# Another order on the way to the first expert, the gates spread by GpSimd, and the next tokens' low parts between two weight low parts

## The chip, the cores and the metric

The kernel runs on one core of a Trainium2 chip. The metric is the device time of one execution in microseconds (us); lower is better. The engines are TensorE (PE, with PEld for its weight loads), VectorE (DVE), ScalarE (ACT), GpSimd (POOL) and SyncE (SP), which here only issues transfers.

## The reference

One layer of a decoder over 1024 tokens of 1024 channels, in float32. Two mixers (an RG-LRU and an S5 scan), a cross-attention into 256 memory tokens, then a mixture of experts: each token goes to its top 4 of 32 experts, each a clamped SwiGLU with weights of 1024x2048 and 1024x1024.

```
logits = xt @ router_w + router_b
top_val, top_idx = lax.top_k(logits, TOP_K)
gates = jax.nn.softmax(top_val, axis=-1)
...
def clamped_swiglu_expert(xb, w_gu, b_gu, w_down, b_down):
    gu = xb @ w_gu + b_gu
    g, u = gu[:, :D_FF], gu[:, D_FF:]
    ...
    h = (u + 1.0) * (g * jax.nn.sigmoid(SWIGLU_ALPHA * g))
    return h @ w_down + b_down
...
y = jnp.zeros((n, d), xt.dtype).at[slot_tok].add(yb.reshape(n_slots, d) * slot_w[:, None])
```

## The kernel before

Every engine has its own program, written out by hand in the order in which it runs; semaphores alone join them. A matrix product of the experts is done in three passes over float32r parts: ACT casts a weight tile of 1 MB to its high part (WH), DVE subtracts to get the low part (WL, `low_weights`), and TensorE multiplies high by high, low by high and high by low. Tokens are treated alike: TensorE transposes them into PSUM, ACT keeps the high part (XEH, `keep_tokens`), DVE the low part (XEL, `low_tokens`); the hidden rows give HTH and HTL (`low_hidden`).

**The loop** runs over items, of which 36 have work. An item is one expert's gate/up product for up to 128 tokens (one tile), or 192 (two tiles, a wide expert), together with the down product of the item before. TensorE's order in one turn is: four pairs of gate/up passes (the bias matmul L976 opens each pair, then L984, L988), the first half of the next tokens' transposes (L942), two down parts (L1005, L1012), the second half of the next tokens' transposes, the hidden transposes of half 0 (L1037), two down parts, the hidden transposes of half 1. The latter write the PSUM banks in which the second half of the next tokens stood, so they wait for `xel_done`, DVE's low part of that half. The next turn's first matmul is L976, which waits for `htl_done`, the hidden rows' low part of half 0. The loop is two loops, one of four turns inside another (`items`).

At the turn's end DVE does, in this order: low weight 8, low weight 9 (the next expert's first two gate/up tiles), the next tokens' second half, the hidden rows' low part of half 0, low weights 10 and 11. SP loads a weight tile into a slot when `gu_low` says that the low part of the tile in it is done.

**The way to the first expert.** After the last router product DVE works out the slots: the item list (ITM, which every engine waits for as `itm_done`), the positions, a one-hot of their rows (OHR, 128x3072; ACT scales it in eight parts into IDR), a one-hot of their columns (OHC, `slot_columns`), which TensorE multiplies with IDR into the list of tokens by slot (`list_done`), and the gates (GF: softmax weights spread over the experts, 128x256). GF goes to DRAM by SP (`gf_done`), ahead of SP's loop; GF3 is three copies of it, for the very end. The low weights 1 to 3 stand in the place of OHC and IDR, so they wait for the list. TensorE's program starts its loop behind the evacuation of the last bank (EBS), the first tokens' transposes and the list.

Of the kernel before, what the change touches and what calls it, by code (L numbers as in the profile page):

```python
# [13 lines left out]
F32 = mybir.dt.float32  # L14
# [7 lines left out]
P = 128  # L22
# [7 lines left out]
def build(nc, A, out):  # L30
    D = A["w_in"].shape[0]
    T = A["x"].shape[1]
    L = T // P
# [11 lines left out]
    TOPK = 4  # L45
# [14 lines left out]
    with ctx:  # L60
# [3 lines left out]
        def sem(name):  # L64
            return ctx.enter_context(nc.semaphore(name))
# [192 lines left out]
        def raw_gu(j):  # L258
            return raw((j + 2) % 6)
# [105 lines left out]
        def units_read(eng, kind):  # L365
# [30 lines left out]
        gexp_in, gexp_done, gf_done, gf_out = sem("gexp_in"), sem("gexp_done"), sem("gf_done"), sem("gf_out")  # L396
        hot0_done, idx0_done, idr_done, list_done, tab_done = (
            sem("hot0_done"), sem("idx0_done"), sem("idr_done"), sem("list_done"), sem("tab_done"))
        ohr_done, rw_done = sem("ohr_done"), sem("rw_done")
        acc_out, ids_done, gs_in = sem("acc_out"), sem("ids_done"), sem("gs_in")  # L400
        ms_done, itm_done, ite_done = sem("ms_done"), sem("itm_done"), sem("ite_done")
        hot_done, idx_done = sem("hot_done"), sem("idx_done")
# [668 lines left out]
        def _(act):  # L1071
# [244 lines left out]
            def keep_tokens(half, tiles):  # L1316
                for t in range(tiles):
                    n = HP if t else P
                    ins = nc.scalar.copy(XEH[:, 4 * half:4 * half + 4, t * P:t * P + n],
                                         PS[:, 2 * half + t, :].rearrange("p (k s) -> p k s", k=4)[:, :, 0:n])  # L1320
                ins.then_inc(xeh_done, 1)

            act.sem_inc(dn_high, 4)
            act.wait_ge(ohr_done, 1)
            for l in range(L):
                hot = OHR.rearrange("p (j l) r -> p j l r", l=L)[:, :, l, :]
                nc.scalar.activation(IDR[l // 4][:, :, l % 4, :], hot, ACT.Copy, scale=TOKF[:, l:l + 1]).then_inc(idr_done, 1)
            for half in range(2):
                act.wait_ge(xt_filled, half + 1)
                keep_tokens(half, 2)  # L1330
            act.wait_ge(gf_done, 1)
            nc.scalar.copy(GF3.rearrange("p l (r e) -> p l r e", r=3), GF.unsqueeze(2).to_broadcast([P, L, 3, E])) \
                .then_inc(gf3_done, 1)
            act.wait_ge(itm_done, 1)
            counts = Counts(act, "act")
            with items(act, counts, each=True) as i:
# [131 lines left out]
        def _(dve):  # L1468
# [392 lines left out]
            for t in range(2):  # L1861
                if t:
# [35 lines left out]
            d(v.tensor_reduce(K0[:, 3:4], IT2, AX.X, add))  # L1898
            ts(K0[:, 3:4], K0[:, 3:4], float(E - 1), None, ALU.min)
            ts(DIAG, ident[:], K0[:, 3:4], None, mul, s=ite_done)  # L1900
            tt(OHS, OH, SL.unsqueeze(1).to_broadcast([P, TOPK, L * E]), mul)
            d(v.tensor_reduce(POSf, OHS.rearrange("p j (l e) -> p (j l) e", l=L), AX.X, add))
            ts(PRW, POSf, 1.0 / P, 0.5 / P - 0.5, mul, add)
            ts(PRW, PRW, 1.5 * 2 ** 23, None, add)
            ts(PRW, PRW, 1.5 * 2 ** 23, None, sub)
            stt(PCL, PRW, -float(P), POSf, mul, add)
            dve.wait_ge(acc_out, 16 * (L + 1))
            v.tensor_tensor(OHR, PRW.unsqueeze(2).to_broadcast([P, TOPK * L, NROW]),
                            IOF[:, 0:NROW].unsqueeze(1).to_broadcast([P, TOPK * L, NROW]), ALU.is_equal).then_inc(ohr_done, 1)
            wait_filled(dve, ("itm",))  # L1910
            evac(dve, v.tensor_copy(ITM3[:, 0:2, 1:P + 1],
                                    bank(("itm",))[0:1, 0:2 * P].rearrange("o (r c) -> o r c", r=2)), ("itm",), own=True)
            dve.sem_inc(itm_done, 1)
            wait_filled(dve, ("eb",))
            evac(dve, v.tensor_copy(EBS, bank(("eb",))[:, 0:NROW]), ("eb",), own=True)
            def slot_columns(h):
                ns = slice(2 * L * h, 2 * L * (h + 1))
                v.tensor_tensor(OHC[:, ns, :], PCL[:, ns].unsqueeze(2).to_broadcast([P, 2 * L, P]),
                                IOF[:, :].unsqueeze(1).to_broadcast([P, 2 * L, P]), ALU.is_equal).then_inc(hot_done, 1)

            def gates():
                dve.wait_ge(gexp_done, 1)
                d(v.tensor_reduce(MXT[:, 0:L], GW, AX.X, add))
                d(v.reciprocal(MXT[:, 0:L], MXT[:, 0:L]))
                tt(GW, GW, MXT[:, 0:L].unsqueeze(2).to_broadcast([P, L, TOPK]), mul)
                for j in range(TOPK):
                    tt(GT1 if j else GF, OH4[:, j], GW[:, :, j:j + 1].to_broadcast([P, L, E]), mul)
                    if j:
                        tt(GF, GF, GT1, add, s=gf_done if j == TOPK - 1 else dve_step)

            def low_tokens(half, tiles):
                for t in range(tiles):
                    n = HP if t else P
                    o = XEH[:, 4 * half:4 * half + 4, P + HP:W] if t else XEL[:, 4 * half:4 * half + 4, 0:P]
                    hi = XEH[:, 4 * half:4 * half + 4, t * P:t * P + n].bitcast(F32)
                    ins = v.tensor_tensor(o, PS[:, 2 * half + t, :].rearrange("p (k s) -> p k s", k=4)[:, :, 0:n], hi, sub)
                ins.then_inc(xel_done, 1)

            def low_weights(s, src, done):
                v.tensor_tensor(WL[:, s, :], src, WH[:, s, :].bitcast(F32), sub).then_inc(done, 1)  # L1940

            dve.sem_inc(dn_low, 8)
            dve.sem_inc(htl_done, 2)
            for j in range(4):
                dve.wait_ge(gu_high, j + 1)
                low_weights(j, raw_gu(j), gu_low)
                if j == 0:
                    slot_columns(0)
                    slot_columns(1)
                    for half in range(2):  # L1950
                        dve.wait_ge(xeh_done, half + 1)
                        low_tokens(half, 2)
                    gates()
                    dve.wait_ge(list_done, 1)
                    ts(IDXF, PS[:, 7, 0:NROW], 1.0, 0.0, sub, ALU.max)
                    d(v.tensor_copy(IDX[:, 0:NROW], IDXF), idx_done)
            ts(SCF, PS[:, 7, 0:NROW], 0.5, DUM, ALU.is_lt, mul)
# [5 lines left out]
            with items(dve, counts) as i:  # L1963
# [87 lines left out]

                def weights_and_tokens(tiles):
                    gate_up_low(8)
                    gate_up_low(9)
                    next_tokens(1)(tiles)

                def no_tokens():
                    last_low(0)
# [40 lines left out]
        def _(pool):  # L2099
# [112 lines left out]
            pool.sem_inc(ys_free, 1)  # L2212
            pool.sem_inc(y_done, 1)
            g.tensor_copy(SELR[:, 0:P], SELT[:, 0:1].to_broadcast([P, P])).then_inc(sel_done, 1)
            pool.wait_ge(itm_done, 1)
            n_1 = entry(pool, 1, 2, W)
            pool.wait_ge(xt_filled, 2)
# [73 lines left out]
```

## Time and profile before

| | us |
|---|---|
| median of 3 runs | 2253.53 (2251.64 to 2256.22) |
| the profiled execution: its span, from first to last instruction | 2253.7 |
| PE busy | 2157.0 (96%) |
| PEld busy | 1693.2 (75%) |
| DVE busy | 1619.9 (72%) |
| ACT busy | 1271.3 (56%) |
| POOL busy | 458.0 (20%) |

The profiled execution has no time besides its span; the span lies inside the range of the runs. Busy times are of one profiled execution. The end of a matmul is modelled, so short gaps between matmuls are read better from start to start. All times of a timeline count from the span's start.

### The profile page before, as it was taken

What the parts mean: (1) busy time and instruction counts of PE and PEld (TensorE: products, weight loads), DVE (VectorE), ACT (ScalarE), POOL (GpSimd) and SP (SyncE); (2) the same over time, 40 slices, a digit from 0 to 9 for tenths busy, and PEclk for the clock granted to TensorE, in tenths of its full rate; (3) what the DMA queues carried; (4) which work ended last, traced back from release to release, by engine and by line L of the source; (5) the groups of instructions that cost most, each with busy time, mean ns of one, the idle gap of its engine ahead of it and who ended that gap; (6) DMA issues with size and microseconds to landing.
All of it is one profiled execution on the core that took longest, in us unless ns stands there. A gap on an engine that the chain in (4) does not pass through costs nothing.

```text
span 2253.7 us, 32977 instructions
## 1 busy us (share of the span) xinstructions
PE 2157.0 (96%) x9642; PEld 1693.2 (75%) x9643; DVE 1619.9 (72%) x1572; ACT 1271.3 (56%) x1213; POOL 458.0 (20%) x357
## 2 busy tenths in 40 slices
PE   7999999999996899999999999999999999999996
PEld 4454877887785688887787888788878787887873
DVE  5645743405537899787879977997889779997793
ACT  3135342514313577666667756775677667775673
POOL 0792000000000122122231222321322122222210
PEclk9999999999997899999999999999999999999997
DMA  5102332111233799899899979998999799997895
GB/s 174 38 1 96 105 131 83 38 38 38 68 129 110 295 377 374 302 329 310 283 316 375 377 270 317 377 375 309 325 327 363 271 319 372 378 378 269 306 344 174
DMA packets 233653, 555.72 MB, mean 247 GB/s; under 512 B 19972, under 2 KB 20200, under 8 KB 232392
## 3 DMA queue, kind: packets, MB, share of 16 engines
q1 hardware_dynamic: 218448, 512.41, 62.0%
q0 software_dynamic: 13200, 42.37, 7.5%
q10 hardware_dynamic: 1960, 0.35, 0.1%
q8 instruction: 28, 0.46, 0.1%
q14 instruction: 17, 0.14, 0.0%
HBM read 518.12 MB, written 33.69 MB: 245 GB/s over the span
## 4 chain that ended last, share of the span: by engine, by line
PE 80%; issue 8%; DVE 6%; ACT 3%; DVEq 1%; DMA 1%; ACTq 1%; POOLq 0%
PE PS L984 21%; PE PS L648 20%; PE PS L988 11%; PE PS L1005 9%; PE PS L1012 5%; PE PS L806 4%; PE PS L846 4%; DVE WL L1940 2%; PE PS L976 2%; PE PS L1037 1%; ACT WH L1344 1%; PE PS L942 1%; PE PS L666 1%; PE PS L1065 1%; ACT WH L1367 1%
## 5 line engine op out<-in xcount | busy, mean ns | idle before, releaser
L1940 DVE TENSOR_TENSOR WL<-WA,WH 128x2048 fp32r<-128x2048 f32 x288 | 651.5, 2284 | 69.7 <-ACT WH L1367 48.8
L1940 DVE TENSOR_TENSOR WL<-H,WH 128x2048 fp32r<-128x2048 f32 x144 | 329.2, 2286 | 84.0 <-ACT WH L1344 63.5
L984 PE MATMUL PS<-WH,XEH 128*128 128x512 f32 x1344 | 362.5, 392 | 3.4 <-DVE WL L1940 3.4
L988 PE MATMUL PS<-WL,XEH 128*128 128x512 f32 x1344 | 352.1, 390 | 0.0
L1367 ACT CAST WH<-WA 128x2048 fp32r<-128x2048 f32 x140 | 267.2, 1910 | 146.1 <-PE PS L1012 145.3
L984 PE MATMUL PS<-WH,XEL 128*128 128x512 f32 x1152 | 310.3, 391 | 0.0
L984 PEld LDWEIGHTS PS<-WH,XEH 128*128 128x128 f32 x1344 | 253.5, 189 | 55.3 <-DVE WL L1940 3.8
L988 PEld LDWEIGHTS PS<-WL,XEH 128*128 128x128 f32 x1344 | 252.9, 188 | 52.9
L984 PEld LDWEIGHTS PS<-WH,XEL 128*128 128x128 f32 x1152 | 217.8, 189 | 46.2
L1005 PE MATMUL PS<-WH,HTH 128*128 128x512 f32 x672 | 187.6, 401 | 4.6 <-DVE HTL L2040 4.6
L1344 ACT CAST WH<-H 128x2048 fp32r<-128x2048 f32 x72 | 136.9, 1909 | 89.9 <-PE PS L988 87.3
L1012 PE MATMUL PS<-WL,HTH 128*128 128x512 f32 x672 | 176.4, 390 | 0.0
L1349 ACT CAST WH<-WA 128x2048 fp32r<-128x2048 f32 x70 | 133.7, 1912 | 73.7 <-PE PS L988 73.7
L2249 POOL CAST SELR<-WA 128x128 fp32r x35 | 29.1, 832 | 713.2 <-PE PS L942 713.2
L648 PE MATMUL PS<-XT,WB 128*128 128x512 f32 (+1 forms) x512 | 166.2, 486 | 1.6 <-DVE XT L1499 1.6
L1344 ACT CAST WH<-WA 128x2048 fp32r<-128x2048 f32 x72 | 136.6, 1907 | 36.7 <-PE PS L988 36.7
L1005 PE MATMUL PS<-WH,HTL 128*128 128x512 f32 x576 | 155.4, 392 | 0.0
L1349 ACT CAST WH<-H 128x2048 fp32r<-128x2048 f32 x70 | 132.9, 1908 | 33.5 <-PE PS L988 31.9
L648 PEld LDWEIGHTS PS<-XT,WB 128*128 128x128 f32 x512 | 97.1, 190 | 69.2 <-issue 62.6
L1012 PEld LDWEIGHTS PS<-WL,HTH 128*128 128x128 f32 x672 | 126.6, 188 | 26.8
L2265 POOL DMA_INDIRECT y_acc<-WA x42 | 93.7, 2230 | 246.1 <-ACT WA L1424 155.6
L1005 PEld LDWEIGHTS PS<-WH,HTH 128*128 128x128 f32 x672 | 121.4, 189 | 26.4 <-DVE WL L1940 4.8
(333 smaller groups left out, 2915.3 us busy)
## 6 DMA issues: line engine op xcount, KB each, us to landing
WA<-in_exp_w_gu SPq DMA_DIRECT2D x216, 1024.0 KB, 7.4
H<-in_exp_w_gu SPq DMA_DIRECT2D x72, 1024.0 KB, 6.5
WA<-in_exp_w_down SPq DMA_DIRECT2D x72, 1024.0 KB, 9.0
H<-in_exp_w_down SPq DMA_DIRECT2D x72, 1024.0 KB, 8.0
WB<-in_xa_wkv SPq DMA_DIRECT2D x4, 2048.0 KB, 7.9
WB<-in_w_in SPq DMA_DIRECT2D x3, 2048.0 KB, 9.5
y_acc<-H SPq DMA_DIRECT2D x9, 512.0 KB, 2.6
H<-in_x SPq DMA_DIRECT2D x4, 1024.0 KB, 6.0
```

The lines of the kernel that those rows point to most:

```text
L648: return nc.tensor.matmul(o, a, b, start=(k == 0), stop=(k == n - 1))
L806: ins = nc.tensor.matmul(o, x(k), w(k), start=k_first and n == 0, stop=k_last and n == 3 * len(ks) - 1)
L846: ins = nc.tensor.matmul(o, w[:, k, j * P:(j + 1) * P], x[:, :, k, :], start=n == 0, stop=n == 3 * K - 1)
L984: nc.tensor.matmul(PS[:, 2 * h + t, :], x[:, KT4 * half + k, t * P:(t + 1) * P], WH[:, j % 4, k * HALF:(k + 1) * HALF], start=False, stop= ...
L988: ins = nc.tensor.matmul(PS[:, 2 * h + t, :], XEH[:, KT4 * half + k, t * P:(t + 1) * P], WL[:, j % 4, k * HALF:(k + 1) * HALF], start=Fals ...
L1005: nc.tensor.matmul(PS[:, 4 + 2 * t + c, :], hx[:, 2 * m + k, t * P:(t + 1) * P], WH[:, m, k * D + c * HALF:k * D + (c + 1) * HALF], start= ...
L1012: ins = nc.tensor.matmul(PS[:, 4 + 2 * t + c, :], HTH[:, 2 * m + k, t * P:(t + 1) * P], WL[:, m, k * D + c * HALF:k * D + (c + 1) * HALF], ...
L1344: nc.scalar.copy(WH[:, s, :], raw_gu(4 + s)).then_inc(gu_high, 1)
L1349: nc.scalar.copy(WH[:, m, :], raw_dn(m)).then_inc(dn_high, 1)
L1367: nc.scalar.copy(WH[:, s, :], raw_gu(s)).then_inc(gu_high, 1)
L1940: v.tensor_tensor(WL[:, s, :], src, WH[:, s, :].bitcast(F32), sub).then_inc(done, 1)
L2265: g.indirect_dma_start(out=y_acc[:, :], out_offset=bass.IndirectOffsetOnAxis(ap=IDS[0:n, t, 0:1], axis=0), in_=YS[0:n, t, :], in_offset=No ...
```

## The change

Four things. On DVE's way to the first expert, the item list's evacuation, low weight 0 and EBS now stand ahead of OHS, the positions and OHR. The gates' spreading over the experts (four products, three sums) and GF3 go from DVE and ACT to GpSimd; DVE keeps the normalisation. ACT keeps the first tokens' high parts before it scales OHR. And low weight 1 goes ahead of the conversion of the list to indices. In the loop, DVE does the next tokens' second half between low weights 8 and 9.

```diff
@@ ACT
             act.sem_inc(dn_high, 4)
+            for half in range(2):
+                act.wait_ge(xt_filled, half + 1)
+                keep_tokens(half, 2)
             act.wait_ge(ohr_done, 1)
             for l in range(L):
...
-            for half in range(2):
-                act.wait_ge(xt_filled, half + 1)
-                keep_tokens(half, 2)
-            act.wait_ge(gf_done, 1)
-            nc.scalar.copy(GF3.rearrange("p l (r e) -> p l r e", r=3), GF.unsqueeze(2).to_broadcast([P, L, 3, E])) \
-                .then_inc(gf3_done, 1)
@@ DVE, way to the first expert
             ts(DIAG, ident[:], K0[:, 3:4], None, mul, s=ite_done)
+            wait_filled(dve, ("itm",))
+            evac(dve, v.tensor_copy(ITM3[:, 0:2, 1:P + 1], ...
+            dve.sem_inc(itm_done, 1)
+            dve.wait_ge(gu_high, 1)
+            low_weights(0, raw_gu(0), gu_low)
+            dve.wait_ge(acc_out, 16 * (L + 1))
+            wait_filled(dve, ("eb",))
+            evac(dve, v.tensor_copy(EBS, bank(("eb",))[:, 0:NROW]), ("eb",), own=True)
             tt(OHS, OH, SL.unsqueeze(1).to_broadcast([P, TOPK, L * E]), mul)
...
-                for j in range(TOPK):
-                    tt(GT1 if j else GF, OH4[:, j], GW[:, :, j:j + 1].to_broadcast([P, L, E]), mul)
-                    if j:
-                        tt(GF, GF, GT1, add, s=gf_done if j == TOPK - 1 else dve_step)
...
-            for j in range(4):
+            slot_columns(0)
+            slot_columns(1)
+            for half in range(2):
+                dve.wait_ge(xeh_done, half + 1)
+                low_tokens(half, 2)
+            normal_gates()
+            dve.wait_ge(list_done, 1)
+            for j in range(1, 4):
                 dve.wait_ge(gu_high, j + 1)
                 low_weights(j, raw_gu(j), gu_low)
-                if j == 0:
...
+                if j == 1:
                     ts(IDXF, PS[:, 7, 0:NROW], 1.0, 0.0, sub, ALU.max)
                     d(v.tensor_copy(IDX[:, 0:NROW], IDXF), idx_done)
@@ DVE, in the loop
                 def weights_and_tokens(tiles):
                     gate_up_low(8)
+                    next_tokens(1)(tiles)
                     gate_up_low(9)
-                    next_tokens(1)(tiles)
@@ POOL, ahead of its first wait for itm_done
+            pool.wait_ge(gw_done, 1)
+            for j in range(TOPK):
+                tt(GT1 if j else GF, OH.rearrange("p j (l e) -> p j l e", l=L)[:, j],
+                   GW[:, :, j:j + 1].to_broadcast([P, L, E]), mul)
+                if j:
+                    tt(GF, GF, GT1, add, s=gf_done if j == TOPK - 1 else pool_step)
+            pool.wait_ge(idr_done, L)
+            g.tensor_copy(GF3.rearrange("p l (r e) -> p l r e", r=3), GF.unsqueeze(2).to_broadcast([P, L, 3, E])) \
+                .then_inc(gf3_done, 1)
```

DVE, the way to the first expert, before (OHS is the first row, H<-YT,iota_row is OHR, WA<-PS the item list's evacuation, H<-PS is EBS, WL<-WA,WH low weight 0, WL<-YT,iota_row the slot columns):

```order
L1475 TENSOR_TENSOR YT<-WA 128x1024 [waits ite_done]
L1902 TENSOR_REDUCE YT<-YT 128x32 [waits dve_step]
L1478 TENSOR_SCALAR YT<-YT 128x32 [waits dve_step] x3
L1481 SCALAR_TENSOR_TENSOR YT<-YT 128x32 [waits dve_step]
L1908 TENSOR_TENSOR H<-YT,iota_row 128x3072 [waits acc_out,dve_step]
L1911 CAST WA<-PS 1x2x128 [waits bank3_filled]
L1915 COPY H<-PS 128x96 [waits bank3_emptied,bank4_filled]
L1940 TENSOR_TENSOR WL<-WA,WH 128x2048 [waits bank4_emptied,gu_high]
L1918 TENSOR_TENSOR WL<-YT,iota_row 128x2048 x2
```

The same place after:

```order
L1902 CAST WA<-PS 1x2x128 [waits bank3_filled,ite_done]
L1899 TENSOR_TENSOR WL<-WA,WH 128x2048 [waits bank3_emptied,gu_high]
L1909 COPY H<-PS 128x96 [waits bank4_filled,acc_out]
L1472 TENSOR_TENSOR YT<-WA 128x1024 [waits bank4_emptied]
L1911 TENSOR_REDUCE YT<-YT 128x32 [waits dve_step]
L1475 TENSOR_SCALAR YT<-YT 128x32 [waits dve_step] x3
L1478 SCALAR_TENSOR_TENSOR YT<-YT 128x32 [waits dve_step]
L1916 TENSOR_TENSOR H<-YT,iota_row 128x3072 [waits dve_step]
L1920 TENSOR_TENSOR WL<-YT,iota_row 128x2048 x2
```

The two evacuations and low weight 0 have moved from behind OHR to the front.

GpSimd after, between the first gather of tokens and the second (before, the second row here is followed at once by the last one):

```order
L2204 DMA WA<-xn_rows,WA 64x1024
L2209 CAST SELR<-WA 128x128
L2102 TENSOR_TENSOR H<-WA,sm 128x256 [waits gw_done]
L2102 TENSOR_TENSOR WA<-WA,sm 128x256 [waits pool_step]
L2102 TENSOR_TENSOR H<-H,WA 128x256 [waits pool_step]
...
L2217 COPY H<-H 128x768 [waits idr_done,gf_done]
L491 TENSOR_LOAD WA [waits itm_done]
```

Seven products and sums and the copy into GF3 now stand ahead of the item list's first load.

DVE in the loop, a next expert of one tile, before (WL<-WA,WH are low weights 8 and 9, then 10 and 11 follow after the hidden rows):

```order
L1969 ISA
L1940 TENSOR_TENSOR WL<-WA,WH 128x2048 [waits gu_high]
L1969 REGISTER_ALU
L1940 TENSOR_TENSOR WL<-WA,WH 128x2048 [waits gu_high]
L2029 ISA
L1936 TENSOR_TENSOR XEL<-PS,XEH 128x4x128 [waits xeh_done]
L450 UNCONDITIONAL_BRANCH
```

The same place after:

```order
L1964 ISA
L1899 TENSOR_TENSOR WL<-WA,WH 128x2048 [waits gu_high]
L2024 ISA
L1934 TENSOR_TENSOR XEL<-PS,XEH 128x4x128 [waits xeh_done]
L1964 REGISTER_ALU
L1899 TENSOR_TENSOR WL<-WA,WH 128x2048 [waits gu_high]
L450 UNCONDITIONAL_BRANCH
```

The tokens' low part stands one low weight earlier; the rows behind are the same.

## Rows read from the trace of the kernel before

**Rows 1.** The core's span and mean granted clock.
```profile
core 0: 2253.7 us, clock 0.983
```

**Rows 2.** Busy time of PE, PEld, DVE, ACT, POOL; granted clock, DMA share, GB/s.
```profile
722.00:725.00 3.00, 3.00 (x17) 3.00 (x17) 3.00 (x3) 2.38 (x6) 0.00 (x0) 0.55 0.00 0
725.00:729.00 4.00, 3.87 (x35) 3.75 (x33) 3.97 (x7) 0.86 (x2) 0.00 (x0) 1.00 0.01 4
1000.00:2200.00 1200.00, 1173.04 (x5381) 962.48 (x5379) 1007.16 (x717) 823.67 (x618) 286.24 (x187) 1.00 0.94 331
```

**Rows 3.** TensorE's waits from 790 to 2195: us in total, times, longest.
```profile
PE PS L976 <- issue: 11.6, 15, 1.4
PE PS L1037 <- DVE XEL L1936: 8.7, 11, 1.0
```

**Rows 4.** Timeline, end of an ordinary turn: start, us, engine, line, operation.
```profile
834.81 4.48 DVE L1940 TENSOR_TENSOR WL<-WA,WH 128x2048 fp32r<-128x2048 f32 x2
...
836.50 0.59 ACT L1319 CAST XEH<-PS 128x512 fp32r<-128x512 f32 x1
...
839.21 0.68 DVE L1936 TENSOR_TENSOR XEL<-PS,XEH 128x512 fp32r<-128x512 f32 x1
...
839.81 0.68 DVE L2040 TENSOR_TENSOR HTL<-PS,HTH 128x512 fp32r<-128x512 f32 x1
...
840.84 0.60 PE L1037 MATMUL PS<-ident,WA 128*128 128x128 f32 x4
...
841.49 0.50 PE L976 MATMUL PS<-BIASR,SELR 128*128 128x512 f32 x1
```

**Rows 5.** Timeline, end of a turn with down products of two tiles.
```profile
1004.37 0.68 DVE L1936 TENSOR_TENSOR XEL<-PS,XEH 128x512 fp32r<-128x512 f32 x1
...
1009.98 0.60 PE L1037 MATMUL PS<-ident,WA 128*128 128x128 f32 x4
...
1010.33 0.47 PE L976 MATMUL PS<-BIASR,SELR 128*128 128x512 f32 x1
```

**Rows 6.** Timeline, end of an ordinary turn that also leaves the inner loop.
```profile
877.75 0.49 PE L976 MATMUL PS<-BIASR,SELR 128*128 128x512 f32 x1 [0.55 <-issue]
```

**Rows 7.** Timeline, end of a wide expert's turn.
```profile
965.97 1.09 PE L1037 MATMUL PS<-ident,WA 128*128 128x128 f32 x8 [0.62 <-DVE XEL L1936]
966.44 0.40 DVE L2040 TENSOR_TENSOR HTH<-PS,HTH 128x256 fp32r<-128x256 f32 x1
...
967.68 0.50 PE L976 MATMUL PS<-BIASR,SELR 128*128 128x512 f32 x1 [0.62 <-issue]
```

**Rows 8.** Timelines on the way to the first expert; last, the loads' landing.
```profile
715.97 3.36 DVE L1908 TENSOR_TENSOR H<-YT,iota_row 128x3072 f32<-128x3072 f32 x1
719.36 2.13 ACT L1327 ACTIVATE WL<-H,sm 128x384 fp32r<-128x384 f32 x4 [7.72 <-DVE H L1908]
721.88 3.31 PE L942 MATMUL PS<-ident,WA 128*128 128x128 f32 x16 [8.42 <-issue]
722.50 4.49 DVE L1918 TENSOR_TENSOR WL<-YT,iota_row 128x2048 fp32r<-128x2048 f32 x2
...
729.44 0.43 DVE L1475 TENSOR_TENSOR H<-WA,sm 128x256 f32<-128x256 f32 x1
...
733.19 6.69 DVE L1940 TENSOR_TENSOR WL<-WA,WH 128x2048 fp32r<-128x2048 f32 x3
...
736.52 19.75 SPq L556 DMA_DIRECT2D WA<-in_exp_w_gu  x6
746.62 3.70 ACT L1344 CAST WH<-WA 128x2048 fp32r<-128x2048 f32 x2
DMA to landing us min/median/max: 5.2/7.4/9.7
```

**Rows 9.** GpSimd: one form of its operations, and one copy in time.
```profile
L2107 POOL TENSOR_TENSOR WA<-WA,sm 128x256 f32<-128x256 f32 x4 | 2.5, 620 | 0.3
734.12 1.40 POOL L2220 COPY WA<-WA 128x2 int32 x1 [22.41 <-DVE WA L1956]
```

More of the change, by code:

```diff
@@ L398, in build @@
             sem("hot0_done"), sem("idx0_done"), sem("idr_done"), sem("list_done"), sem("tab_done"))
-        ohr_done, rw_done = sem("ohr_done"), sem("rw_done")
+        ohr_done, rw_done, gw_done = sem("ohr_done"), sem("rw_done"), sem("gw_done")
         acc_out, ids_done, gs_in = sem("acc_out"), sem("ids_done"), sem("gs_in")
@@ L1900, in _, with low_weights @@
             ts(DIAG, ident[:], K0[:, 3:4], None, mul, s=ite_done)
+            def low_weights(s, src, done):
+                v.tensor_tensor(WL[:, s, :], src, WH[:, s, :].bitcast(F32), sub).then_inc(done, 1)
+            wait_filled(dve, ("itm",))
+            evac(dve, v.tensor_copy(ITM3[:, 0:2, 1:P + 1],
+                                    bank(("itm",))[0:1, 0:2 * P].rearrange("o (r c) -> o r c", r=2)), ("itm",), own=True)
+            dve.sem_inc(itm_done, 1)
[4 more added lines that the diff above has]
+            evac(dve, v.tensor_copy(EBS, bank(("eb",))[:, 0:NROW]), ("eb",), own=True)
             tt(OHS, OH, SL.unsqueeze(1).to_broadcast([P, TOPK, L * E]), mul)
@@ L1906, in _ @@
             stt(PCL, PRW, -float(P), POSf, mul, add)
-            dve.wait_ge(acc_out, 16 * (L + 1))
             v.tensor_tensor(OHR, PRW.unsqueeze(2).to_broadcast([P, TOPK * L, NROW]),
                             IOF[:, 0:NROW].unsqueeze(1).to_broadcast([P, TOPK * L, NROW]), ALU.is_equal).then_inc(ohr_done, 1)
[L1910 to L1915, printed above, removed]
             def slot_columns(h):
@@ L1919, in slot_columns, with normal_gates @@
                                 IOF[:, :].unsqueeze(1).to_broadcast([P, 2 * L, P]), ALU.is_equal).then_inc(hot_done, 1)
-            def gates():
+            def normal_gates():
                 dve.wait_ge(gexp_done, 1)
@@ L1924, in gates @@
                 d(v.reciprocal(MXT[:, 0:L], MXT[:, 0:L]))
-                tt(GW, GW, MXT[:, 0:L].unsqueeze(2).to_broadcast([P, L, TOPK]), mul)
-                for j in range(TOPK):
-                    tt(GT1 if j else GF, OH4[:, j], GW[:, :, j:j + 1].to_broadcast([P, L, E]), mul)
-                    if j:
-                        tt(GF, GF, GT1, add, s=gf_done if j == TOPK - 1 else dve_step)
+                tt(GW, GW, MXT[:, 0:L].unsqueeze(2).to_broadcast([P, L, TOPK]), mul, s=gw_done)
             def low_tokens(half, tiles):
@@ L1937, in low_tokens @@
                 ins.then_inc(xel_done, 1)
-            def low_weights(s, src, done):
-                v.tensor_tensor(WL[:, s, :], src, WH[:, s, :].bitcast(F32), sub).then_inc(done, 1)
             dve.sem_inc(dn_low, 8)
             dve.sem_inc(htl_done, 2)
-            for j in range(4):
+            slot_columns(0)
[6 more added lines that the diff above has]
+            for j in range(1, 4):
                 dve.wait_ge(gu_high, j + 1)
                 low_weights(j, raw_gu(j), gu_low)
-                if j == 0:
[L1948 to L1954, printed above, removed]
+                if j == 1:
                     ts(IDXF, PS[:, 7, 0:NROW], 1.0, 0.0, sub, ALU.max)
```

## The prediction

> **What bounds it now.** I read the view by stretch first. In the loop over experts TensorE is busy 1173 of 1200 us at the full granted clock, 2.4 GHz, and DMA 0.94 of the time [rows 2]. So the loop, about 1,460 of the 2253.7 us of span [rows 1], goes at TensorE's pace, and only its gaps can be won. The list of TensorE's waits in the loop then says which gaps there are [rows 3]: 8.7 us for DVE's low part of the next tokens (XEL, L1936; one more wait of this kind is filed under XEH), and 11.6 us before the bias matmul L976 that opens an expert, put down to "issue", a time in which nothing that is seen was missing.
>
> The timelines say what that issue time is. In an ordinary turn [rows 4] the tokens' low part ends at 839.89 and the four hidden transposes L1037, which need it, start at 840.84, so the page shows no wait. Yet the bias matmul starts at 841.49, 0.65 after the transposes' start. In [rows 5] the low part was ready at 1005.05, five microseconds early, and the bias matmul follows the same four transposes after 0.35. The 0.30 more fits one cause: TensorE's sequencer comes to the transposes early, stands at the semaphore of the low part, and only then works through the end of one turn and the head of the next (registers and branches). From the low part's end to the bias matmul it is 1.60 in [rows 4], and 1.71 in [rows 7] from the transposes that the low part released. The matmuls already queued cover part of it. Every fourth turn leaves the inner loop too, and there the profile shows 0.55 of idle [rows 6] where the ordinary turn shows 0.05 (840.84 + 0.60 to 841.49). Beside the wide experts (two tiles) the low part is later than TensorE itself: 0.62 of visible wait and 0.62 of issue [rows 7].
>
> The way to the first expert is another regime: one chain through DVE, ACT and TensorE [rows 8].
>
> **The change in the loop.** DVE now does low weight 8, then the second half's tokens, then low weight 9. No work is added. The tokens' low part comes one low weight earlier, 4.48/2 = 2.2 us [rows 4]. Its other input, ACT's high part L1319, ends at 837.09, just when low weight 8 does (834.81 + 2.28), so DVE stalls by 0.1 at most. Low weight 9 becomes 0.6 later; it is used in the second pass of the next expert, and SP's load that waits for it 0.6 later too. The hidden rows' low part, the next thing that the bias matmul needs, stays where it was, after all three. It is what is late next.
>
> The gain, turn by turn, over the 34 turns with a next expert after the first turn:
> - nine already look like [rows 5]: nothing.
> - ten ordinary ones like [rows 4]: 0.30 each, 3.0 us. The hidden low part allows it: it ends at 840.49 (839.81 + 0.68), and the bias matmul would come at 841.19.
> - three ordinary ones at a group's end: 0.5 more idle than that [rows 6], so 0.8 each, 2.4 us.
> - twelve beside wide experts, the waits of [rows 3]: there the hidden low part takes over. In [rows 7] it ends at 966.84 and the bias matmul starts at 967.68; with 0.15 for the semaphore 0.7 is won. Six are of this kind, 4.3 us. For the other six the same interval gives 0.8, and 1.2 to 1.4 at the two group ends: 5.8 us. Together 10.1.
>
> Sum 15.5 us. The first turn, which does no down product, gives 0.7 more by the same rule.
>
> **The change on the way to the first expert.** Before, DVE built OHS, the positions and OHR up to 719.33 (715.97 + 3.36), then came the evacuations that release TensorE, whose token transposes begin at 721.88, 2.5 after OHR's end [rows 8]. Now the item list's evacuation, low weight 0 (2.28) and EBS go first: about 3.0 us for the three. The whole of OHS to OHR, 6.7 us, no longer lies ahead of the transposes; low weight 0 does. They begin near 717.5. OHR ends near 722.4, the slot columns (4.49) near 726.9. ACT's eight scaled copies, four in 2.13, end near 726.6. The list matmuls therefore start near 726.8 instead of 724.95. They follow 6 us without TensorE work. Before, the transposes after 8 idle us ran at a granted clock of 0.55, and the list at 1.00 in 4 us [rows 2]. At full clock the list would end at 730.8, at half clock throughout at 734.8. The clock came back after about 3 us of work, so I take 732.3 (before 728.9). Both ends bound the term.
>
> DVE had seven gate instructions of 0.42 to 0.43 from 729.44 on, 3.2 us with the gaps; they go to GpSimd, and in their place DVE waits for the list. Its three low weights start at 732.3 instead of 733.19, and the first of them now precedes the index conversion. TensorE's second pass starts with the first of them, about 1 us earlier than before, but TensorE is then held by DVE's next low weights and the table, 10 us as before: free of GpSimd, DVE would reach the first expert's fifth low weight 0.5 earlier than before.
>
> GpSimd is not free. A product of 128x256 takes 0.62 there [rows 9]; seven with 0.08 between them, the sums somewhat dearer, make 5.2 us, from 729.4 to 734.6 instead of DVE's 732.65. From 732.3 DVE runs low weights. A two-element copy on GpSimd that began at 734.12 took 1.40 and ended with the low weight that DVE had under way (733.19 + 2.29) [rows 8, 9]. So the last three gate instructions, which start at or after 732.3, each wait for a weight part or delay one. I bound their end by 736.9, where they slip in between DVE's instructions, and 741.3, where they get one gap after each low weight. The Trainium skill, "SBUF — State Buffer", section "Who interferes with whom", says that a DVE instruction with two SBUF inputs shuts out a GpSimd one that reads SBUF for its whole length. By that rule the late end, 741.3, is the likelier, and the trace's 1.40 us copy agrees.
>
> Behind it stands SP: its queue waits for the finished gates before it loads the first expert's last two weight tiles. The loads left from 736.52 on, 3.9 after the gates' end (729.44 + 7 x 0.46), and landed 5.2 and 9.7 after their issue, at 741.7 and 746.9; ACT wanted the first at 746.62 [rows 8]. So 4.9 us of lateness is free for the first. With gates at 736.9 (4.3 late) the loads cost about nothing, and with 741.3 (8.6 late) 3.7 us. Add 0 to 1 us by which GpSimd holds up DVE. Cost of this part: from -0.5 to +5; I take +2.5. The spread gates' copy (GF3) and the next tokens' gather come later too, with over 10 us to spare; ACT, rid of GF3, has nothing to do there.
>
> Sum: 2253.7 + 2.5 - 0.7 - 15.5 = 2240.0. The span agrees with the median of the runs, 2253.5, to 0.2, so **2240 us**, 0.6% less.
>
> **Rivals.**
> - *Only visible waits count.* The 0.3 of ordinary turns is the matmuls' modelled end, not the sequencer. For it: the profile gives those turns only 0.05 of idle. Against: 0.55 at a group's end. Then 10.1 + 0.7 - 2.5 = 8.3 are won: 2245.5. The Trainium skill, "Advanced Engine Details and Errata", section "Sequencer and Instruction Queues", lets the sequencer queue further engine instructions past a waiting one, up to 64 on TensorE; by that alone the turn's overhead would be hidden already, as this rival has it, and the 1.60 and 1.71 us from low part to bias matmul speak against it. Chance 0.22.
> - *The gain is handed on.* The hidden low part or the loads, at a DMA share of 0.94, take back what the tokens give; the head costs 2.5. 2253 to 2257. Against: the nine early turns run without a gap and their loads are in time. Chance 0.12.
> - *Slower: ACT's high part is late at its new place.* DVE now stands still for L1319 with low weight 9 and the hidden low part queued behind it, and TensorE waits for the latter. Margin in an ordinary turn: the 0.7 between 840.49 and 841.19. If ACT came 1.3 us after low weight 8, the hidden low part would end at 841.8 and the bias matmul start at 841.9, 0.4 later than now, in 23 of the turns: +9 us, and with the head's 1.8, 2264.5. It decides from about 0.9 us of stall per turn on. Against: ACT follows TensorE at a fixed distance. Chance 0.06; 0.02 more for a head worse than 15 us.
> - *Gates at their worst with the full loop gain.* 741.3 and 5 us: 2242.5. It lies in the forecast's own range.
>
> **Numbers.** My forecast 0.58, visible waits 0.22, handed on 0.12, slower 0.08. A measurement of this kernel tells about 0.2%, 4.5 us, from no change. Faster: 0.58 + 0.22 = 0.80, less 0.01 that the second case gives when its head is at the dear end; same 0.12; slower 0.09. The forecast's own range is 2236 to 2244. For 8 times in 10 it goes from 2235 (the head at its best, 3.0 under the sum, and 2 more for the twelve turns) to 2248 (the second case with the dear head).
>
> **What would show it.** Right: waits L1037 on XEL gone from the loop, L976's issue time from 11.6 to under 4, beside wide experts a short wait of L976 for the hidden low part, and 0.35 from transposes to bias matmul in ordinary turns. In the head: transposes near 717.5, the list near 726.8 and partly at a lower clock, the seven GpSimd instructions stretched beside low weights, SP's first load of the loop at 741 to 745, and a wait of ACT for it. Wrong: a DVE wait for XEH in each turn, ACT waits for weights in the loop, or 0.65 left in turns whose low part is early.

## The result, and the profile after

The changed kernel takes 2235.74 us (median of 5 runs, 2234.69 to 2237.43), the kernel before 2253.53 (5 runs, 2251.64 to 2257.78). The ratio is 0.9918, with a 95% interval from 0.9906 to 0.993: 17.8 us less, where 13.5 were forecast. The profiled execution took 2235.84 us and has a span of 2234.1, so 1.7 us lie outside the span.

TensorE's waits in the loop, of the changed kernel, from 790 to 2175 (us in total, times, longest), answer to [rows 3]:

```profile
PE PS L976 <- DVE HTL L2035: 7.0, 6, 1.2
PE PS L976 <- DVE HTH L2035: 4.6, 6, 0.8
PE PS L976 <- DVE WA L1975: 2.7, 6, 0.7
PE PS L976 <- DVE WA L1998: 1.6, 6, 0.3
```

Both lines of [rows 3] are gone: no wait of L1037 for XEL, and none of the 11.6 us of "issue". The twelve turns beside wide experts now wait for the hidden rows' low part. (The last two lines were there before.)

The timeline of the changed kernel at the end of the same ordinary turn as [rows 4]:

```profile
834.10 2.28 DVE L1899 TENSOR_TENSOR WL<-WA,WH 128x2048 fp32r<-128x2048 f32 x1
...
835.79 0.58 ACT L1319 CAST XEH<-PS 128x512 fp32r<-128x512 f32 x1
...
836.41 0.69 DVE L1934 TENSOR_TENSOR XEL<-PS,XEH 128x512 fp32r<-128x512 f32 x1
...
837.01 2.28 DVE L1899 TENSOR_TENSOR WL<-WA,WH 128x2048 fp32r<-128x2048 f32 x1
...
839.21 0.68 DVE L2035 TENSOR_TENSOR HTL<-PS,HTH 128x512 fp32r<-128x512 f32 x1
...
840.13 0.60 PE L1037 MATMUL PS<-ident,WA 128*128 128x128 f32 x4
...
840.48 0.47 PE L976 MATMUL PS<-BIASR,SELR 128*128 128x512 f32 x1
```

The low part XEL is ready at 837.10, three microseconds ahead of the transposes L1037, and the bias matmul follows their start by 0.35 instead of 0.65. DVE does not stand for ACT: low weight 8 ends at 836.38, XEL starts at 836.41.

The traces also hold the instructions of TensorE's sequencer (PEldq; nanoseconds, then the start in us). The last one ahead of the hidden transposes (L1032) and the first one behind them (L471), at the end of this turn before:

```profile
L1032 PEldq ALU_OP  x1: 36/36/36, 837.3 to 837.3; - x1
L471 PEldq FUSED_REGOPS  x1: 105/105/105, 840.0 to 840.0; - x1
```

and in the changed kernel:

```profile
L1032 PEldq ALU_OP  x1: 36/36/36, 836.6 to 836.6; - x1
L471 PEldq FUSED_REGOPS  x1: 105/105/105, 837.2 to 837.2; - x1
```

Before, the sequencer ran nothing for 2.6 us and went on right behind the low part's end (839.89); all registers and branches of the turn's end and the next turn's head came after that. In the turn of [rows 5], where the low part is early, the same two instructions start at 1006.7 and 1006.8, three microseconds ahead of the transposes. In the changed kernel the sequencer goes on 3.0 us ahead of the transposes (837.2 and 840.13). At the head of the next turn it then stands for the hidden rows' low part (ready at 839.89; its next instruction, L967, starts at 839.9), with little left to do before the bias matmul.

At the end of the wide turn (as [rows 7]) the transposes come without a wait, and the bias matmul starts 0.14 after the hidden low part's end (964.57 + 0.40):

```profile
963.30 1.03 PE L1037 MATMUL PS<-ident,WA 128*128 128x128 f32 x8
...
964.57 0.40 DVE L2035 TENSOR_TENSOR HTH<-PS,HTH 128x256 fp32r<-128x256 f32 x1
...
965.11 0.49 PE L976 MATMUL PS<-BIASR,SELR 128*128 128x512 f32 x1 [0.77 <-DVE HTH L2035]
```

The way to the first expert, of the changed kernel (as [rows 8]):

```profile
710.82 0.29 DVE L1475 TENSOR_SCALAR YT<-ident,YT 128x128 f32<-128x128 f32 x1
...
711.70 2.29 DVE L1899 TENSOR_TENSOR WL<-WA,WH 128x2048 fp32r<-128x2048 f32 x1
...
715.98 0.88 PE L942 MATMUL PS<-ident,WA 128*128 128x128 f32 x3 [3.96 <-issue]
...
725.18 1.09 PE L648 MATMUL PS<-WL 128*128 128x96 f32 x4 [5.55 <-ACT HTL L1330]
...
727.84 0.63 POOL L2102 TENSOR_TENSOR H<-WA,sm 128x256 f32<-128x256 f32 x1 [17.56 <-DVE sm L1472]
...
732.04 0.76 PE L976 MATMUL PS<-BIASR,SELR 128*128 128x512 f32 x1
...
732.26 0.73 POOL L2102 TENSOR_TENSOR H<-H,WA 128x256 f32<-128x256 f32 x1
732.34 2.81 DVE L1899 TENSOR_TENSOR WL<-WA,WH 128x2048 fp32r<-128x2048 f32 x1 [4.59 <-PE PS L648]
...
733.07 2.76 POOL L2217 COPY H<-H 128x768 f32<-128x768 f32 x1
...
736.90 1.11 SPq L556 DMA_DIRECT2D WA<-in_exp_w_gu  x2
...
743.82 2.29 DVE L1899 TENSOR_TENSOR WL<-H,WH 128x2048 fp32r<-128x2048 f32 x1 [1.97 <-issue]
```

Windows of the same stretch (columns as in [rows 2]):

```profile
716.00:720.00 4.00, 3.62 (x16) 3.22 (x16) 3.83 (x6) 1.20 (x3) 0.00 (x0) 0.50 0.01 2
725.00:732.00 7.00, 6.82 (x32) 6.83 (x33) 2.68 (x8) 0.12 (x1) 3.77 (x6) 0.50 0.01 2
732.00:737.60 5.60, 5.60 (x15) 4.44 (x15) 5.19 (x4) 0.00 (x0) 4.60 (x4) 0.50 0.07 25
```

The reader is to see three things. The transposes come early, as forecast. But the granted clock stays at 0.50, 1.2 GHz, through the whole list and the first expert's first matmuls; in [rows 2] the list had 1.00. And GpSimd's gates run while DVE stands at the list: from 727.84 to 732.99, only the last beside a low weight. SP's loads leave at 736.90, 0.4 later in the span than before and 1.8 later counted from DVE's DIAG row (26.1 and 24.3), and ACT takes the first of the two tiles at 747.28 without a wait.

**Where the time went.** I cut each trace at two starts: DVE's DIAG row (710.82 above; the changed code begins behind it) and the first bias matmul of item 1. A third cut is the last one-tile bias matmul L976 of the loop.

| us | span's start to DIAG | DIAG to item 1 | item 1 to last bias | from there to the end |
|---|---|---|---|---|
| before | 712.3 | 55.6 | 1411.6 | 74.3 |
| changed | 710.8 | 57.0 | 1393.8 | 72.5 |

The loop gives 17.8 us. The head with the first turn costs 1.4. The 1.4 us ahead of DIAG and the 1.8 behind the loop are not put down to the change: no instruction there is changed, and the kernels below move by as much there (710.4 to 712.9 to DIAG, 72.0 to 74.2 at the end). So the profiled spans differ by 19.6 us and the medians by 17.8.

### The profile page after: what moved, and what is told of

It is laid out like the page before. It is cut to its first block, busy times and chain, and to the rows that moved or that the text cites. A ratio compares the mean times of both kernels' runs of the same rounds, so it can differ in the third digit from the quotient of the medians.

```text
span 2234.1 us, 32979 instructions
## 1 busy us (share of the span) xinstructions
PE 2151.1 (96%) x9642; PEld 1694.5 (76%) x9643; DVE 1620.4 (73%) x1565; ACT 1270.4 (57%) x1212; POOL 460.5 (21%) x365
## 4 chain that ended last, share of the span: by engine, by line
PE 80%; issue 8%; DVE 6%; ACT 3%; DVEq 1%; ACTq 1%; DMA 1%; POOLq 0%
PE PS L984 21%; PE PS L648 20%; PE PS L988 11%; PE PS L1005 9%; PE PS L1012 5%; PE PS L806 4%; PE PS L846 4%; DVE WL L1899 2%; PE PS L976 2%; ACT WH L1341 1%; PE PS L942 1%; PE PS L666 1%; PE PS L1037 1%; PE PS L1065 1%; ACT WH L1364 1%
```

## The experiments

### One part at a time

Loop alone: the kernel before with

```
                     gate_up_low(8)
+                    next_tokens(1)(tiles)
                     gate_up_low(9)
-                    next_tokens(1)(tiles)
```

> Only the loop part of the change is made (next tokens' low part between low weights 8 and 9); the way to the first expert is that of before. Theory of the record, as the trace after sizes it (late low part holds TensorE's sequencer as well as TensorE): the loop is worth 16 to 18 us, so 2236 to 2238 us, and ordinary turns take 35.4 us instead of 35.7. Rival, only waits that the profile shows count: 10 us, 2243 us. Rival, the head does part of the work: 2240 or more.

Head alone: the changed kernel with these lines back in the old order.

> Only the head of the change is made (order on DVE and ACT, gate spreading on GpSimd); the loop is that of before. Theory: the head costs between nothing and 2.5 us, 2253.5 to 2256 us. Rival, the head is itself a gain because the token transposes come 6 us earlier: 2250 us or less. The loop's waits should be those of before: L976 issue 11 to 12 us, L1037 for XEL 8 to 9 us.

Measured: the loop alone 2235.38 us (0.9917, 0.9902 to 0.9931). The head alone 2258.75 (1.002, 1.0011 to 1.0029), with L976's issue time at 11.7 and L1037's for XEL at 8.7, as before. So the loop part carries the whole gain, as forecast, and the head is a loss, in the median a larger one than I expected. By the cuts, DIAG to item 1 takes 54.9 in the loop-only kernel, 0.7 less than before (the first turn), and 57.75 in the head-only one, 2.15 more than before. With the new loop the head costs 57.0 - 54.9 = 2.1 as well.

Two numbers don't add up yet: with the new loop the head costs 0.4 us of the median, with the old one 4.8. I come back to both.

### Where the gate spreading runs

Two kernels with the new loop. The first is the changed kernel with the gates on DVE and GF3 on ACT again:

```
-                tt(GW, GW, MXT..., mul, s=gw_done)
+                tt(GW, GW, MXT..., mul)
+                for j in range(TOPK):
+                    tt(GT1 if j else GF, OH4[:, j], GW[:, :, j:j + 1]..., mul)
+                    if j:
+                        tt(GF, GF, GT1, add, ...)
```

> The changed kernel with the seven gate instructions back on DVE, behind the normalisation and ahead of the wait for the list, and the gate copy GF3 back on ACT; order and loop as changed. Theory A, from the trace after (DVE stood 4.6 us at the list, and the gates take 3.2 us there): the place of the gates makes no difference, 2235.0 to 2236.5 us. Theory of the record, that gates on GpSimd hold up DVE and SP: this kernel is 1 to 3 us faster, 2233 to 2235. Rival, that spreading on GpSimd is what pays: 2 to 4 us slower, 2238 to 2240.

The second has the order of before and only moves the gates and GF3 to GpSimd:

> The head's order of before with only the gate spreading moved to GpSimd, and the loop as changed. Here the list ends near 729 and DVE goes straight on to its low weights, so that all of GpSimd's gate instructions fall beside low weights, which they did not in the changed kernel. If the two engines shut each other out, as the record supposed, the seven take 8 us or more instead of 5.2, their end is near 738 to 741, and SP's loads follow late: 2236 to 2240 us, against the loop alone no gain. If they don't, DVE starts its low weights 3.7 us earlier and the time is 1 to 3 us below that of the loop alone, 2233 to 2235.

Measured: gates on DVE 2236.31 (0.9919, 0.9905 to 0.9933), the same as the changed kernel within what can be told. Its trace tells more: DVE's low weights start 21.5 us after DIAG as in the changed kernel, but none is stretched (2.29), the index conversion takes 0.5 instead of 0.8, and item 1 starts 56.1 after DIAG instead of 57.0. So the gates and GF3 on GpSimd cost 0.9 there, which the median doesn't show. Gates on GpSimd in the old order 2239.86 (0.9933, 0.992 to 0.9947), 4.5 more than the loop alone on the same chip. Its timelines of GpSimd, DVE, SP and ACT show the whole chain that the prediction feared:

```profile
730.15 0.63 POOL L2100 TENSOR_TENSOR H<-WA,sm 128x256 f32<-128x256 f32 x1 [17.77 <-DVE sm L1472]
...
731.57 2.66 POOL L2100 TENSOR_TENSOR H<-H,WA 128x256 f32<-128x256 f32 x1
734.32 2.56 POOL L2100 TENSOR_TENSOR WA<-WA,sm 128x256 f32<-128x256 f32 x1
736.96 2.66 POOL L2100 TENSOR_TENSOR H<-H,WA 128x256 f32<-128x256 f32 x1
739.70 0.63 POOL L2100 TENSOR_TENSOR WA<-WA,sm 128x256 f32<-128x256 f32 x1
...
741.21 0.82 POOL L2215 COPY H<-H 128x768 f32<-128x768 f32 x1
...
730.88 8.14 DVE L1933 TENSOR_TENSOR WL<-WA,WH 128x2048 fp32r<-128x2048 f32 x3
...
741.17 0.32 SPq L582 DMA_DIRECT2D gate_rows<-H  x1
745.04 14.75 SPq L556 DMA_DIRECT2D WA<-in_exp_w_gu  x5
...
750.44 1.91 ACT L1341 CAST WH<-WA 128x2048 fp32r<-128x2048 f32 x1 [3.60 <-DMA WA<-in_exp_w_gu]
```

A gate instruction that takes 0.63 to 0.73 alone takes 2.6 beside a low weight; one gets in per low weight, and each low weight is lengthened as well: three take 8.14 instead of 6.69 [rows 8]. The gates end at 741.14, the loads leave at 745.04, ACT waits 3.60 us for the first. (The Trainium skill, "SBUF — State Buffer", section "Who interferes with whom", says that a DVE instruction with two SBUF inputs contends with a GpSimd one that reads SBUF. The trace agrees, 2.66 us instead of 0.63 to 0.73. The copy GF3 is a second case: 2.76 in the changed kernel, where a low weight was running, and 0.82 here, where none was.) So the mechanism is real; the changed kernel escapes most of it, because there the list holds DVE up.

### TensorE kept at work ahead of the list

The changed kernel with 36 transposes of the identity, into a bank that is free, in the 5.6 us ahead of the list; they compute nothing that is used:

```
+            for n in range(36):
+                nc.tensor.transpose(PS[:, 5, 0:P], ident[:], ident[:])
             pe.wait_ge(idr_done, L)
```

> The changed kernel with 36 transposes of the identity into a free PSUM bank between the token transposes and the list, where TensorE stands 5.6 us; they compute nothing that is used. Theory A, the head is held by TensorE's half clock: granted full clock when the list starts, the list takes 3.6 instead of 7 us and the first expert's matmuls are at full clock too, DVE's low weights start 2 to 3 us earlier: 2232 to 2234 us. Rival, the list ends earlier but GpSimd's gates, SP's loads or DVE's ten low weights hold the first expert as before: 2235.5 us, no change.

Measured: 2237.54 (0.9938, 0.9924 to 0.9952); by its interval not to be told from the changed kernel (measured on another chip), and not the gain to 2232 to 2234 that I expected. That the clock sets the list's length shows all the same, in this kernel's windows of the extra transposes and of the list:

```profile
720.10:725.90 5.80, 4.68 (x39) 4.44 (x37) 5.80 (x4) 5.02 (x10) 0.00 (x0) 0.92 0.01 1
725.90:730.70 4.80, 4.80 (x32) 4.80 (x32) 2.32 (x7) 0.00 (x0) 2.09 (x4) 0.71 0.01 3
```

With work before it the list begins at full clock, which falls again within it; its matmuls take 4.7 instead of 6.7 us from the first start to the last, and DVE's wait for it 2.64 instead of 4.59. Of this 1.0 reaches item 1 (DIAG to item 1 55.9, changed kernel 57.0), since now two gate sums collide with low weights (2.66 and 2.67 us). Then the loop took 1.2 more (1395.0 against 1393.8): in most of the turns beside wide experts the bias matmul came 0.1 to 0.2 later after the hidden low part. What causes that I have not found.

### Is it the sequencer?

The forecast rests on the reading that a late low part holds TensorE's sequencer, so that the turn's registers and branches lie open behind it. Four compare-and-branch steps more at the end of each turn, without engine work, in either kernel:

```
                 by_tiles(pe, n_i, hidden_transposes(1))
+                for n in range(4):
+                    with pe.If_cmp(n_i, -1 - n, "IS_GT"):
+                        pe.wait_ge(bias_done, 1)
```

> The kernel before with four extra compare-and-branch steps on TensorE's sequencer at the end of each turn, no engine work; each about 0.3 us. Theory A, the late low part holds the sequencer, whose turn overhead then lies open in 25 of 34 turns: 1.0 to 1.3 us in each, +25 to +32 us, 2279 to 2286, and 0.3 more becomes about 1.5 between the transposes and the bias matmul of an ordinary turn. Rival, the 0.3 and 0.55 are only the modelled ends of matmuls and the sequencer runs ahead: within 3 us of before.

> The changed kernel with the same four extra steps of TensorE's sequencer. Theory A, the low part is there before the sequencer comes to the transposes, so the extra steps lie under matmuls already queued: 0 to 5 us (the twelve turns beside wide experts have the least cover), 2236 to 2241 us. Rival, sequencer work costs the same in both kernels, as plain time: +25 us or more here as well.

Measured: in the kernel before 2305.16 us (1.024, 1.0222 to 1.0258), 53 over the kernel before on the same chip (2251.78); in the changed one 2239.38 (0.9943, 0.993 to 0.9957), 3 to 4 us over the changed kernel, which was measured on another chip. In the traces the part from item 1 to the last bias grows by 46.9 us in one and by 3.7 in the other, of which 1.6 is a stretch at the lower clock (below). The kernel before with the steps, an ordinary turn:

```profile
841.88 0.68 DVE L1939 TENSOR_TENSOR XEL<-PS,XEH 128x512 fp32r<-128x512 f32 x1
...
843.51 0.60 PE L1037 MATMUL PS<-ident,WA 128*128 128x128 f32 x4
...
845.56 0.50 PE L976 MATMUL PS<-BIASR,SELR 128*128 128x512 f32 x1 [1.45 <-issue]
```

and the changed one with the steps:

```profile
840.15 0.60 PE L1037 MATMUL PS<-ident,WA 128*128 128x128 f32 x4
...
840.50 0.47 PE L976 MATMUL PS<-BIASR,SELR 128*128 128x512 f32 x1
```

In the first, 2.05 us lie between the starts instead of 0.65. In the second it is 0.35 still. Turn by turn, half-clock stretches left out, the kernel before becomes 1.2 to 1.5 us longer in 27 of 34 turns and 0.8 in item 1's own; the six that stay are turns like [rows 5]. That is 39 us, and five more half-clock stretches than before add 8. I had expected 25 to 32 in all. The steps alone are above it, since one costs about 0.35 and not 0.3 (it also holds a wait for a semaphore that was reached long before), and since three more turns, those that lead into a wide expert, turn out to be only just covered; the stretches I had not counted at all. The rival (modelled ends) would have had nothing in either.

### The next step of the same kind

What the bias matmul waits for beside wide experts is DVE's order again. In the changed kernel the first half's hidden low part is put ahead of low weight 9:

```
                     gate_up_low(8)
                     next_tokens(1)(tiles)
-                    gate_up_low(9)
...
                 by_tiles(dve, n_i, low_hidden(0))
                 with dve.If_cmp(n_n, 0, "IS_GT"):
+                    gate_up_low(9)
                     gate_up_low(10)
```

> The changed kernel with one more step of the same kind: the first half's hidden low part also goes ahead of low weight 9, since it is what the bias matmul waits for beside wide experts (11.6 us in 12 turns after the change). Theory A, the next bound is only DVE's order: these waits fall to the 0.35 of early turns, up to 11 us less, 2225 to 2230 us. Rival, DVE now stands for ACT's high part of the hidden rows with three low weights queued behind it in each turn, DVE is over 0.9 busy there, and the lateness goes to the low weights and through them to SP's loads: 2236 us or more, with TensorE waits for low weights.

Measured: 2229.07 (0.9901, 0.9885 to 0.9916), some 7 us less. Twelve turns lose 0.8 to 1.4 each, but in nine of the turns behind them 0.6 to 0.7 comes back, at the second bias matmul, which waits for the second half's hidden low part (L976 on HTL). That led to the last round, on one chip, with the changed kernel beside them:

> The changed kernel itself, on the chip of the next three, as their measure. Expected as before: 2235 to 2237 us, runs within 3 us of each other, no or one half-clock stretch in the loop.

> The head of before, with the tokens' and the first half's hidden low part both ahead of low weight 9. If head and loop add up, the loop is that of the kernel with the changed head (i1 to the last bias 1387 us) and the head's 2.1 us less, of which 0.4 to 1.4 arrive at the end: 2227.5 to 2228.5 us. Rival, the head's gain is given back at the clock's next step: same as with the changed head, 2229.

> As the kernel before it in this list, and the second half's hidden low part ahead of low weight 11 as well. With one step fewer the first expert after a wide one gave back 0.6 to 0.7 us in 12 turns, at the second bias matmul, waiting for this low part. Theory, DVE's order is still the bound there: 5 to 7 us less, 2221 to 2223 us. Rival, low weight 11 is then as late as the low part was, or ACT and the loads: no change.

Measured: the changed kernel 2236.24 (2235.12 to 2237.44); with the old head and this step 2225.78 (0.9877, 0.9862 to 0.9892); with the second half's part ahead of low weight 11 as well 2221.47 (0.9855, 0.984 to 0.987). That is 14.8 us below the changed kernel, and the waits of TensorE in its loop are down to

```profile
PE PS L976 <- DVE WA L1980: 5.6, 6, 1.2
PE PS L976 <- DVE WA L2003: 1.5, 6, 0.3
PE PS L976 <- issue: 0.4, 1, 0.4
```

where DVE's gate minimum (L1980) now takes 2.9 more than the 2.7 it had: nine turns gained 0.6 by the last step, and six gave 0.5 back there, which is why it brought 4.3 us where I had expected 5 to 7. The old head fared better than I expected: DIAG to item 1 takes 53.6 us, 2.1 under the kernel with the changed head and the same loop (55.7), and the median is 3.3 lower (another chip), more than the 0.4 that the head cost above.

### The head with the old loop, once more

> The head of the change with the old loop once more, on another chip, since its 2258.8 us stood 4.9 above before, while the same head cost 0.4 with the new loop. Theory, its surplus are half-clock stretches in the loop (about 1.6 us each) that the long pauses of the old loop meet by chance: the runs spread over 5 us or more, the lowest is within 3 us of the lowest of before. Rival, the head costs 4 to 5 us with the old loop in every run: all of them lie above 2256 and the trace shows where.

Measured: 2257.83 (1.0015, 1.0006 to 1.0024), 11 runs from 2254.61 to 2261.07. The spread of over 5 us came as expected, and the rival (all runs above 2256) is out, since four lie below. The lowest is 3.0 above the lowest of before (2251.57), so that even between the lowest runs the head costs 3, not nearly nothing. The windows of this trace show what the spread is made of:

```profile
1051.20:1054.60 3.40, 3.40 (x10) 2.65 (x9) 2.58 (x2) 0.00 (x0) 2.89 (x1) 0.52 1.06 395
1187.70:1191.10 3.40, 3.40 (x10) 2.62 (x9) 3.40 (x3) 0.48 (x1) 2.08 (x1) 0.52 1.04 389
1433.50:1436.90 3.40, 3.40 (x10) 2.70 (x9) 3.32 (x3) 0.27 (x1) 2.29 (x1) 0.53 1.04 386
1887.50:1890.90 3.40, 3.40 (x10) 2.62 (x10) 2.43 (x2) 0.00 (x0) 3.14 (x1) 0.53 1.06 396
2167.20:2170.60 3.40, 3.37 (x8) 2.70 (x9) 3.40 (x2) 0.97 (x1) 1.61 (x1) 0.50 1.05 386
```

Five times in the loop the granted clock is at its lower level, 1.2 GHz, for 3.4 us, each right behind a turn that a late low part had opened widest (1.8 to 2.4 us of idle in two gaps, that end at 1050, 1187, 1433, 1886 and 2167). Each makes its turn 1.6 us longer. The old loop has six such turns; five were followed by a stretch here and one in the earlier head-only trace. From item 1 to the last bias this trace has 1417.3 us and that one 1411.0, and their runs took 2261.07 and 2254.70: the 6.3 to 6.4 us between them are four stretches. The kernel before has one too, behind the bias matmul of 1673.08:

```profile
1673.60:1677.00 3.40, 3.40 (x9) 2.63 (x9) 3.40 (x3) 0.43 (x1) 2.13 (x1) 0.50 1.04 396
```

The kernel before with longer pauses (the four steps) had six, and runs from 2299 to 2311. The changed kernel with the four steps had one. In the traces of the changed kernel, of the loop alone and of all with the new loop and no added steps there is none between 790 us and the last bias, and the runs of each lie within 3.2 us. So the change's loop part also takes away stretches at the lower clock. Why the old loop meets more of them with the new head (medians 3.2 and 4.2 above the lowest run) than with the old one (0.5 to 2.5) stays open.

## Why the prediction was right, and where its terms were off

The measured 2235.74 us lies at the fast end of what was given for 8 times in 10 (2235 to 2248), and 0.3 below the forecast's own range (2236 to 2244).

- **The bound, the sequencer, and what is late next: right.** All three rows said to show it came out: waits on XEL gone, the issue time from 11.6 to nothing, a short wait of L976 for the hidden low part in the twelve turns. The rival "only visible waits count" is refuted by the added branch steps and by the sequencer's own rows.
- **"Sum 15.5 us": mis-sized by 2.3.** The nine early turns changed by 0.02 or less. The ten ordinary ones gave 3.2 (forecast 3.0; 0.6 of it is item 1's own turn, partly at half clock), the group ends 0.82 to 0.85 each, 2.5 (2.4). Those beside wide experts gave 0.71 to 0.79 in six and 0.81 to 1.38 in the other six, 10.4 (10.1). Together 16.2. The other 1.6 is a term that the sum lacks: the half-clock stretch at 1673.6, behind a pause that the change shortens. The mean clock of the window of [rows 2], 1.00 rounded, hides 3.4 us in 1200; the turn from 1673.08 on, 37.84 us long against 36.2 for its like, had shown it.
- **"The first turn gives 0.7 more": right**, 0.73 (55.59 to 54.86 in the loop-only kernel).
- **"Cost of this part ... I take +2.5": size right, 2.1 at item 1, its working only in part.** Counted from DIAG, the list started at 14.4 (forecast 14.5) and the gates on GpSimd at 17.0 (17.1). But the list ran 6.9 us, at half clock throughout, where I took 5.5, so that DVE's low weights started at 21.5, 0.6 later than before instead of 0.9 earlier. This is the step that failed, and it undid the next one: in the 4.59 us that DVE stood there, six of the seven gate instructions ran undisturbed; they ended at 732.99, not between 736.9 and 741.3, and no load was late. The head's price is made of other things than I had in it: 0.6 for the list, 0.5 for a low weight stretched to 2.81 beside GpSimd's last sum and copy, and 0.8 for the index conversion, which now lies between low weights. That is 1.9 of the 2.1 by which the fifth low weight comes later (33.0 after DIAG, before 30.9). With the gates on DVE it comes at 32.1: 0.9 of the 2.1 are GpSimd's, the 0.5 and 0.3 of the conversion among them. That +2.5 lay so near 2.1 is luck.
- **The expected wait of ACT for SP's load: wrong here**, and shown in the kernel with the old order, gates end 741.14 (bound given: 741.3).
- **The rival "ACT's high part is late": came in some turns, and cost nothing.** In ordinary turns DVE stood 0.03 us. But in the six turns like [rows 5] it stands 2.7 us for ACT's high part, more than the 0.9 from which the prediction saw a loss, and 0.5 in the five turns that lead into wide experts (before: none over 0.25). None of these turns became longer: the tokens' low part still starts 7.7 and 4.2 us ahead of the next item's first bias matmul. In the further steps too DVE's order paid.
- **"The span agrees with the median to 0.2": a wrong base.** What lies outside the span was not in sight; in every later profiled execution it was 1.7 to 1.8 us. So the one of before was likely one of 2255.4, some 2 above its median, with two half-clock stretches that the changed kernel's lacks (at 1673.6, and one at 28.4 ahead of DIAG). By the traces the forecast's 13.7 become 19.6: 2.3 more in the loop, 0.4 in head and first turn, and 3.2 outside the change's reach (1.4 ahead of DIAG, 1.8 behind the loop). The medians show 17.8 of them.
- **Where the head's 2.1 went with the new loop.** Item 1 starts 2.1 later than in the loop-only kernel, but the clock comes back at nearly the same moment. The windows of the stretch at half clock end at 771.2 there and at 771.6 here:

The loop-only kernel:

```profile
761.10:771.20 10.10, 6.78 (x17) 5.18 (x18) 9.30 (x7) 5.55 (x6) 1.66 (x1) 0.50 1.05 389
```

and the changed kernel:

```profile
764.90:771.60 6.70, 4.92 (x13) 3.75 (x14) 6.70 (x4) 4.03 (x3) 0.12 (x1) 0.50 1.05 389
```

So item 1 runs 5.7 us at half clock in the first (from 765.53) and 3.8 in the second (from 767.78), which gives back 0.9 of the 2.1, as the cut shows (1394.7 and 1393.8 from item 1 to the last bias). The part behind the last bias gave 0.5 more, for which I have no cause. That is one placing of the clock's changes. With two steps in the loop it went the other way: item 1 ran 3.5 us at half clock with the old head and 4.9 with the changed one, and the head cost 3.3 of the median. With the old loop it cost 4.8 and 3.9 (2258.75 against 2253.91, 2257.83 against 2253.9, each pair on one chip), stretches at the lower clock included. So in medians the head costs 0.4 to 4.8 us, and the traces put it at 2.1 before the clock's changes come in.

## What to carry to other kernels

A wait that the profile shows as nothing can still cost: where an engine's sequencer stands at a semaphore, its loop and branch overhead comes behind the release. Read start to start, compare a turn whose input is early with one whose input is late, look at the sequencer's own rows, and add idle sequencer steps to see whether they are covered. When one late input is moved ahead, ask what the same instruction waits for next and move that too; three such moves were worth 32 us here, the first 18. Work moved to GpSimd was undisturbed here only while DVE wasn't in its low weights, long instructions with two SBUF inputs: place it where DVE waits.

## What was not expected of the hardware

- A pause of 1.8 to 2.4 us in the loop, in two gaps, was followed by 3.4 us at 1.2 GHz in some turns and not in others of the same shape, 1.6 us each, and in one trace more often than in another of the same kernel (five and one). It fits the spread of 7 us of the kernel before (2251.4 to 2258.6 in 17 runs), while the loop alone had 2235.0 to 2236.1.
- A compare and branch with its jump and a met wait on TensorE's sequencer cost about 0.35 us where nothing hid it (1.4 to 1.5 us for four).
- GpSimd and DVE delay each other, not only one the other: a low weight of 2.29 took 2.81 beside a GpSimd sum and the copy behind it, and three took 8.14 instead of 6.69.
